# Twelve filling products behind each level of a chunk inverse and none inside a level, in place of six and six

## The reference, cut to what matters

```python
proj = h @ w_in                      # [256, 2048] @ [2048, about 15,500]; split into a, b, c, gates

def rwkv7_scan(r, decay, k, v, a_vec, b_vec):          # 16 heads of width 64
    def step(state, inp):
        r_t, w_t, k_t, v_t, a_t, b_t = inp
        sa = jnp.einsum('bhij,bhj->bhi', state, a_t)
        state = state * w_t[:, :, None, :] + sa[..., None] * b_t[:, :, None, :] + v_t[..., None] * k_t[:, :, None, :]
        return state, jnp.einsum('bhij,bhj->bhi', state, r_t)
    _, out = lax.scan(step, s0, xs)

merged = sigmoid(ga) * (ya @ w_up_a) + sigmoid(gb) * (yb @ w_up_b) + sigmoid(gc) * (yc @ w_up_c)
return x + merged @ w_o
```

## Time and profile before

| | |
|---|---|
| median of 3 runs | 2583.9 us (2580.15 to 2584.56) |
| the profiled execution, its own time | 2577.35 us |
| its span, first to last instruction | 2575.6 us |
| PE busy | 2498.0 us, 97% |
| DVE busy | 1570.4 us, 61% |
| ACT busy | 1020.9 us, 40% |
| POOL busy | 118.4 us, 5% |
| levels of the scan | 40, between 1973 and 2325 us |

### The profile page before, as it was taken

The page is one execution under the profiler, slowest core; times in us unless marked ns, Lnnn a source line. Parts: engine busy times, 40 slices in busy tenths (PEclk is TensorE's granted clock), DMA queues, the critical chain, the costliest instruction groups (busy, mean ns, idle before and its releaser), DMA issues.

```text
span 2575.6 us, 35191 instructions
## 1 busy us (share of the span) xinstructions
PE 2498.0 (97%) x15104; PEld 2013.6 (78%) x15104; DVE 1570.4 (61%) x1865; ACT 1020.9 (40%) x1254; POOL 118.4 (5%) x220
## 2 busy tenths in 40 slices
PE   6999999998899999999998999999999999999999
PEld 3479988876688888888887888878887777777887
DVE  6777877785655555554445756546954444446864
ACT  2033335563434333333334444443644333333332
POOL 0001211010000000000000000011000000000000
PEclk9999999998899999999999999999999999999999
DMA  9978986553466666655555644466554333336654
GB/s 411 426 258 308 359 323 230 193 205 115 150 234 216 233 215 234 220 212 196 195 190 208 239 165 162 165 228 212 210 195 167 130 132 124 126 122 223 259 180 163
DMA packets 85835, 549.46 MB, mean 213 GB/s; under 512 B 9734, under 2 KB 9894, under 8 KB 33200
## 3 DMA queue, kind: packets, MB, share of 16 engines
q1 hardware_dynamic: 56656, 405.36, 43.6%
q0 software_dynamic: 29024, 141.86, 14.9%
HBM read 531.46 MB, written 12.58 MB: 211 GB/s over the span
## 4 chain that ended last, share of the span: by engine, by line
PE 86%; DVE 7%; DMA 4%; issue 2%; ACT 1%; SPq 0%; DVEq 0%; ACTq 0%
PE psum L2149 39%; PE psum L1020 25%; PE psum L2222 4%; DMA arena<-in_loads 3%; PE psum L2164 2%; PE psum L2397 2%; PE psum L2394 2%; PE psum L2132 2%; DMA weights<-in_loads 1%; DVE arena L2601 1%; PE psum L1148 1%; PE psum L2309 1%; PE psum L1157 1%; PE psum L1155 1%; DVE unit_low L2556 1%
## 5 line engine op out<-in xcount | busy, mean ns | idle before, releaser
L1834 ACT ACTIVATE unit_high<-weights 128x1024 fp32r<-128x1024 f32 (+1 forms) x509 | 719.0, 1428 | 1082.4 <-PE psum L2149 624.1
L2556 DVE TENSOR_TENSOR unit_low<-weights,unit_high 128x2048 fp32r<-128x2048 f32 x221 | 506.1, 2290 | 423.8 <-ACT unit_high L1834 423.7
L1393 DVE TENSOR_TENSOR unit_low<-weights,unit_high 128x1024 fp32r<-128x1024 f32 x240 | 289.1, 1221 | 189.3 <-ACT unit_high L1834 189.2
L2149 PE MATMUL psum<-unit_high,z_high 128*128 128x512 f32 x1152 | 293.6, 398 | 7.2 <-DVE misc L2887 5.4
L2149 PE MATMUL psum<-unit_low,z_high 128*128 128x512 f32 x1152 | 284.9, 389 | 3.4 <-DVE unit_low L2556 3.4
L2149 PE MATMUL psum<-unit_high,z_low 128*128 128x512 f32 x1152 | 285.6, 390 | 0.0
L1020 PE MATMUL psum<-unit_high,z_high 128*128 128x512 f32 x960 | 284.7, 406 | 0.0
L1020 PE MATMUL psum<-unit_high,z_low 128*128 128x512 f32 x960 | 267.1, 394 | 0.0
L1020 PE MATMUL psum<-unit_low,z_high 128*128 128x512 f32 x960 | 264.2, 397 | 1.3 <-DVE unit_low L1393 1.3
L2149 PEld LDWEIGHTS psum<-unit_high,z_high 128*128 128x128 f32 x1152 | 217.4, 191 | 52.2 <-issue 5.9
L2149 PEld LDWEIGHTS psum<-unit_low,z_high 128*128 128x128 f32 x1152 | 216.1, 188 | 49.1 <-DVE unit_low L2556 4.3
(11 more groups left out here) (419 smaller groups left out, 2888.9 us busy)
## 6 DMA issues: line engine op xcount, KB each, us to landing
weights<-in_loads SPq DMA_DIRECT2D x380, 1024.0 KB, 4.8
arena<-in_loads POOLq DMA_DIRECT2D x80, 512.0 KB, 5.9
arena<-in_ada_early POOLq DMA_DIRECT2D x8, 2048.0 KB, 19.2
weights<-in_ada_early POOLq DMA_DIRECT2D x8, 2048.0 KB, 21.7
xn<-in_loads POOLq DMA_DIRECT2D x32, 512.0 KB, 5.4
gates_kept<-h POOLq DMA_DIRECT2D x12, 512.0 KB, 3.7
arena<-gates_kept POOLq DMA_DIRECT2D x12, 512.0 KB, 8.1
weights<-in_loads POOLq DMA_DIRECT2D x11, 512.0 KB, 4.3
```

The source lines that it names most:

```text
L1393: ins = V.tensor_tensor(ring_lo[:, g % RING, c], ring[:, g % RING, c], unit_hi[:, g % 2, c].bitcast(F32), ALU.subtract)
L1834: return nc.scalar.activation(out_, in_, ACT.Copy, scale=scale)
L2149: ins = mm(psum[:, bank + m, 0:width], xk[:, m * P:(m + 1) * P], w[:, k, 0:width], start=(first and i % 8 in (0, 4) and part == 0), stop=( ...
L2556: V.tensor_tensor(ring_lo[:, g % RING], ring[:, g % RING], unit_hi[:, g % 2].bitcast(F32), ALU.subtract)\
```

## The change

The number of filling products behind the first product of a level goes from 6 to 0, and that behind the second from 6 to 12. The sum over a level (12) and over a scan step (120) is as before.

```diff
 STEPS = [("bt", 6), ("g", 8), ("p0", 6)]
 for _l in range(1, 6):
-    STEPS += [(f"p{_l}", 6), (f"d{_l}", 6)]
+    STEPS += [(f"p{_l}", 0), (f"d{_l}", 12)]
 STEPS += [("y", 5), ("ux", 6), ("o1", 6), ("wz", 6), ("s1", 6), ("s2", 6), ("o2", 5)]
 PER_UNIT = 24
```

## The result

The changed kernel took 2592.5 us (median of 5 runs, 2590.75 to 2598.79), the kernel before 2583.3 us in the same session. The ratio is 1.0045, with a 95% interval of 1.0028 to 1.0062: between 7 and 16 us slower. The means of the runs lie 11.6 us apart, which is what the ratio says; the two medians lie 9.2 us apart. A second session gave 1.0046 (1.0032 to 1.0060).

A forecast was written before the change was run, and what follows sets the result against it. PE was taken as the bound. A level became 1.22 + 1.08 + 2.96 = 5.26 us against 4.87 us, 15.6 us more over forty levels; on the base this gave 2598 us, range 2588 to 2609 us for 8 in 10.

The forecast's parts named there:

- What bounds the kernel: Whole kernel: PE, busy 2498.0 of 2575.6 us, sets the time; nothing that ACT or DVE saves counts.
- The hole: Between a level's first and second products: PE waits for ACT's copy into Pm, 0.61 us per level.
- The edges: Filling blocks in a level: one block of twelve lasts 2.96 us, two of six 3.18 us, a gain of 0.22 us.
- The sum: Over the levels: each lasts 5.26 us against 4.87 us, 0.39 us more; forty levels make 15.6 us.
- the likeliest case: The forecast itself, in the levels: 14 to 18 us more, chance 71%; its own range 2591 to 2603 us.
- ACT and DVE at no cost: In the levels: the moved halves on ACT and DVE delay no copy or addition, costed at nothing.
- The clock stayed at 1.00: Rival at the levels: the clock falls once a level, 50 us on top, about 2649 us; chance 5%.
- The edges did give something back: Rival at the filling blocks: the edges give nothing back, loss 24.4 us, about 2608 us; chance 8%.
- ACT's other work: Rival in levels 2 and 4: halves delay 16 copies by up to 1.0 us, 16 us more, about 2615 us; chance 4%.
- the change was measurable: Rival for the whole kernel: no measurable change, a difference under 0.2%, 5.2 us or 0.13 us a level; chance 8%.
- The gain rival: At the block edges, 40 places: vanished edges outweigh the hole, needing 0.74 us for a 0.2% gain; chance 4%.
- The row of 1.93 us: Between blocks of large products: the clock held at 1.00 through 1.93 us idle, so the sum takes 1.00.

The follow-up runs named there:

- One and eleven: One filling product behind a level's first product and eleven behind its second, against the kernel before: ratio 1.0020, scan 381.0 us, 3.4 us more.
- three and nine: Three filling products behind a level's first product and nine behind its second, against the kernel before: ratio 0.9995, scan 377.64 us.
- the version with twelve inside the level: All twelve filling products behind a level's first product, none behind its second, against the kernel before: ratio 1.0088, scan 397.7 us, 20.0 us more.

## Why the prediction was right

**What bounds the kernel.** Right: the scan's 12.3 us arrived whole, with 232.3 us behind the scan in both traces, and ACT's and DVE's spare time counted for nothing.

**The hole.** Right in mechanism and place: in the levels PE waits 40 times, for the copy and for nothing else. ACT starts 0.73 us after the first product and ends after 1.11 us (priced at 1.12 us). The handover from ACT to PE, for which no row existed, was taken at 0.10 us and measured 0.05 to 0.06 us. This is at or just under the lower of the two bounds (0.06 us), and it is the term that was mis-sized: 0.04 us too much in each of 40 levels, 1.7 us.

**The edges.** Right to 0.02 us: the block of twelve lasts 2.94 to 2.95 us (predicted 2.96 us). One and eleven confirms that the price is in the edges.

**The sum.** Predicted 15.6 us in the levels, measured 12.5 us: 0.31 us a level, not 0.39 us. Of the 0.08 us, 0.04 us are the handover, and the rest are hundredths in the copy's end, in the block of twelve and in the length of the level before. So the increase itself lies below the 14 to 18 us of the likeliest case, to which the prediction gave 71%: even with the handover at its lower bound the sum was 14.0 us. That the median still falls between 2591 and 2603 us is owed to the width of the base (2577 to 2585 us), and so far it is luck.

The predicted median, 2598 us, was 5.5 us above the measured one. Of this, 3.1 us are the sum. The base is not the rest: 2598 less 15.6 is 2582.4 us, and the kernel before had a median of 2583.3 us and a mean of 2582.0 us in that session. The other 2.4 us are scatter of the medians, which lie only 9.2 us apart where the means lie 11.6 us and the scans 12.3 us apart.

**ACT and DVE at no cost.** Right: with the wait removed and everything else kept, the scan is shorter than before, which it could not be if a half were in PE's way. In the changed kernel ACT starts each of the 40 copies 0.72 to 0.73 us after the first product, and DVE's addition starts 0.11 to 0.12 us after its product, as before.

**The rivals.** The clock stayed at 1.00 through 40 holes of 0.65 us. The Trainium skill ("TensorE: Matmul & The Clock Gate", section "A second HAM failure mode: psum-queue depth-cycling") reports a kernel whose short idle times made the clock go up and down; the trace does not agree for the holes of this kernel. The edges did give something back, ACT's other work stood in front of no copy, and the change was measurable. The gain rival named the right mechanism, but with a price of 0.22 us against 0.74 us needed. With no wait, the vanished block is worth 0.38 us: besides its own two edges of 0.22 us, the small products also run closer together (the second starts after 0.51 us, not 0.61 us, and lasts 1.03 to 1.04 us, not 1.08 us). I had not counted these, because the hole swallows them in the changed kernel; they matter in the versions with fewer blocks.

## What to carry to other kernels

Filling work between dependent steps has two prices: what it covers and what its edges cost. Count for each place the time that the next step really needs (here 0.65 us for a copy of 0.38 us with its handovers) and give the place at least that much. Beyond it the split made no difference here: six and six and three and nine both had a scan of 377.6 us. What counted then was the number of blocks. Take a block away altogether only where the next step waits for nothing. The change took the block where a wait stood; taking away blocks where none stood gained 0.2% with two blocks a scan step and 0.4% with three.

## What the runs showed that was not expected

The start of the scan, behind 1965 us of program that is the same in all kernels here, scattered from 1963.6 to 1974.8 us over the profiled executions, while the scan of one kernel repeated to the hundredth (389.95 us twice). A comparison of two profiled spans would have given the change 21.4 us; the stretch that it touches gave 12.3 us.

The handover of a result to PE was 0.05 us from ACT's copy, but 0.14 us from DVE's addition at the head of a level. The prediction's two rows had 0.15 and 0.06 us, both from DVE, so the engine alone does not decide it. What does was not tried.

The prediction leaned on a row in which the clock held through an idle time of 1.93 us. At the same place of the program the second profile of the changed kernel shows a longer idle time, 2.82 us, and a clock that fell: the mean over the eight products behind it was 0.60.

```profile
203.44 3.29 PE L2149 MATMUL psum<-unit_low,z_high 128*128 128x512 f32 x8 [2.82 <-DVE unit_low L2556]
203.44:206.53 3.09, 3.09 (x8) 2.42 (x9) 3.05 (x6) 0.00 (x0) 0.00 (x0) 0.60 0.82 330
```

Between these the outcome was mixed. After 2.24 us in the version without the wait the clock stayed at 1.00 (204.62 to 208.49 us); after 2.16 us in the version with twelve inside the level it was 0.50 from 204.50 to 207.50 us. The row of 1.93 us was thus weaker evidence than the prediction took it for. The holes of the change, 0.65 us each, cost no clock in either profile of the changed kernel.
